# Prompt attention's values product in split single-pass form, with both kv heads in one stationary tile and the output weights of the mixer loaded later

## What is computed

```python
def attend(q, k, v, bias, key_valid, sinks):
    s = jnp.einsum('bnqhgd,bnkhd->bnhgqk', q, k).astype(jnp.float32) * (HEAD_DIM ** -0.5) + bias
    ...
    m = jnp.maximum(jnp.max(s, axis=-1, keepdims=True), sink)
    p = jnp.exp(s - m)
    w = p / (jnp.sum(p, axis=-1, keepdims=True) + jnp.exp(sink - m))
    return jnp.einsum('bnhgqk,bnkhd->bnqhgd', w.astype(v.dtype), v)
...
            c, conv_state = short_conv(cg * xi, hist, conv_w[e])
            x = x + jnp.concatenate([a, bg * c], axis=-1) @ mix_w_out[e]
```

## Time and profile before

| | us |
|---|---|
| median of 3 runs | 2050.97 |
| lowest and highest | 2050.38, 2050.98 |
| the profiled execution | 2053.99 |
| its span, first to last instruction | 2052.2 |

### The profile page before, as it was taken

The page is one execution under the profiler, slowest core; times in us unless marked ns, Lnnn a source line. Parts: engine busy times, 40 slices in busy tenths (PEclk is TensorE's granted clock), DMA queues, the critical chain, the costliest instruction groups (busy, mean ns, idle before and its releaser), DMA issues. The chain is left out here.

```text
span 2052.2 us, 34169 instructions
## 1 busy us (share of the span) xinstructions
PE 2036.8 (99%) x13819; PEld 2003.8 (98%) x13819; DVE 1468.8 (72%) x2315; ACT 811.4 (40%) x1352; POOL 533.7 (26%) x366
## 2 busy tenths in 40 slices
PE   9999999999999999999999999999999999999999
PEld 7999999999889999999999999999999999999998
DVE  4896684974666679668487789486677888576685
ACT  6343342442434334334244344243335544333343
POOL 2343232402000034223240234242320045232330
PEclk9999999999999999999999999999999999999999
DMA  6233232333221222323233223323242123323222
GB/s 156 67 83 93 73 98 68 83 98 89 60 63 42 73 68 83 93 73 98 67 83 98 72 57 83 104 62 88 78 126 79 49 60 83 94 72 93 72 57 83
DMA packets 312420, 165.22 MB, mean 81 GB/s; under 512 B 15435, under 2 KB 309527, under 8 KB 312264
## 3 DMA queue, kind: packets, MB, share of 16 engines
q1 hardware_dynamic: 307456, 157.31, 27.9%
q0 software_dynamic: 2576, 4.64, 1.0%
q10 hardware_dynamic: 2232, 1.09, 0.2%
HBM read 159.01 MB, written 4.00 MB: 79 GB/s over the span
## 5 line engine op out<-in xcount | busy, mean ns | idle before, releaser
L522 PE MATMUL psum<-xg_hi,in_hi 128*128 128x320 f32 x1952 | 609.9, 312 | 2.3 <-DVE xg_lo L1379 1.4
L523 PE MATMUL psum<-xg_lo,in_hi 128*128 128x320 f32 x1952 | 603.5, 309 | 0.0
L524 PE MATMUL psum<-xg_hi,in_lo 128*128 128x320 f32 x1952 | 603.4, 309 | 0.0
L522 PE MATMUL psum<-f_hi,f_out_hi 128*128 128x320 f32 x1408 | 436.6, 310 | 3.3 <-DVE f_out_lo L1342 1.5
L523 PE MATMUL psum<-f_lo,f_out_hi 128*128 128x320 f32 x1408 | 435.1, 309 | 0.0
L524 PE MATMUL psum<-f_hi,f_out_lo 128*128 128x320 f32 x1408 | 435.1, 309 | 0.0
L522 PEld LDWEIGHTS psum<-xg_hi,in_hi 128*128 128x128 f32 x1952 | 366.7, 188 | 9.6 <-issue 6.1
L523 PEld LDWEIGHTS psum<-xg_lo,in_hi 128*128 128x128 f32 x1952 | 366.8, 188 | 0.6
L524 PEld LDWEIGHTS psum<-xg_hi,in_lo 128*128 128x128 f32 x1952 | 366.7, 188 | 0.0
L1844 POOL TENSOR_TENSOR sums<-in_raw 128x512 f32<-128x512 f32 x72 | 101.6, 1412 | 733.0 <-DVE in_lo L1346 465.4
L1346 DVE TENSOR_TENSOR in_lo<-in_raw,in_hi 128x1024 fp32r<-128x1024 f32 x144 | 231.8, 1610 | 55.7 <-ACT in_hi L983 55.7
(11 more groups left out here) (225 smaller groups left out, 2845.5 us busy)
## 6 DMA issues: line engine op xcount, KB each, us to landing
in_raw<-in_ffn_w_gate SPq DMA_DIRECT2D x87, 512.0 KB, 4.1
in_raw<-in_ffn_w_up SPq DMA_DIRECT2D x87, 512.0 KB, 5.3
out_raw<-in_ffn_w_down SPq DMA_DIRECT2D x96, 384.0 KB, 3.3
out_raw<-in_ffn_w_down SPq DMA_DIRECT2D x32, 256.0 KB, 2.9
in_raw<-in_mix_w_in SPq DMA_DIRECT2D x14, 512.0 KB, 4.6
out<-y_nat SPq DMA_DIRECT2D x5, 512.0 KB, 3.2
in_raw<-in_mix_w_in SPq DMA_DIRECT2D x8, 256.0 KB, 4.7
out_raw<-in_mix_w_out SPq DMA_DIRECT2D x16, 128.0 KB, 2.8
```

The source lines that it names most:

```text
L522: pe.matmul(dst, w_hi, v_hi, start=first, stop=False)
L523: pe.matmul(dst, w_hi, v_lo, start=False, stop=False)
L524: return pe.matmul(dst, w_lo, v_hi, start=False, stop=last)
```

## The change

The prompt's values products take the split form. v is kept as v_hi and v_lo, turned probabilities as probs_hi0, probs_hi1 and probs_lo0, probs_lo1. ScalarE's two copies now write the high parts; VectorE subtracts them from PSUM in `probs_low(t)`, one subtraction of 512 columns and from unit 2 on one of 256, called inside bias_scores(t+1) between line 1667 and the wait for the exponentials; values(t) waits for it (probs_split). `values_low` splits v the same way during VectorE's step 2. The stationary tile is all 128 columns of v, both heads, so head i's product has 128 output partitions of which 64 are used; head 0 goes to bank 7, head 1 to bank 6, and attn_out reads 64 partitions of each with two instructions per engine instead of one. A copy v_last holds the rows to be stored. Since the new tiles lie over out_raw, the loads of output chunks 0 and 1 move behind mix chunk 8 on SP and wait for the eighth values product and the stored keys and values. The streams' units are as before.

```diff
@@ -206,7 +206,15 @@
         a_hi = over("a_hi", [P, 8, TOKENS], A_HI, F32R)
...
         t2 = over("t2", [P, 2, HALF], arena + 65792)
-        v_nat = over("v_nat", [P, NCHUNK, P], arena)
+        v_hi = over("v_hi", [P, NCHUNK, P], arena, F32R)
+        v_lo = over("v_lo", [P, NCHUNK, P], OUT_HI + 16384, F32R)
+        probs_lo0 = over("probs_lo0", [P, 2, 2, P], OUT_HI + 20480, F32R)
+        probs_lo1 = over("probs_lo1", [P, 2, P], OUT_HI + 22528, F32R)
+        v_last = over("v_last", [P, P], OUT_HI + 23552)
+        probs_hi0 = over("probs_hi0", [P, 2, 2, P], arena + 19488, F32R)
+        probs_hi1 = over("probs_hi1", [P, 2, P], arena + 21536, F32R)
         vs_nat = over("vs_nat", [T_NEW, STREAMS, P], arena + 4096)
...
@@ -343,8 +352,12 @@
         def attn_views(t, a):
...
             if t < NCHUNK:
-                dst = a[:, 0:4, t * CHUNK:(t + 1) * CHUNK].rearrange("p (a g) q -> p a g q", a=2)
-                return [(dst, psum[:, 7, 256:512].rearrange("p (a g q) -> p a g q", a=2, g=2))]
+                views = []
+                for kv in range(2):
+                    r = slice(64 * kv, 64 * kv + 64)
+                    dst = a[r, 0:4, t * CHUNK:(t + 1) * CHUNK].rearrange("p (a g) q -> p a g q", a=2)
+                    views.append((dst, psum[r, 7 - kv, 256:512].rearrange("p (a g q) -> p a g q", a=2, g=2)))
+                return views
             s = 2 * (t - NCHUNK)
@@ -493,9 +506,13 @@
             for tile, lo in ((2, 64), (3, 0), (4, 0)):
...
             start_ffn_out("ffn0", 0, 0)
-            load_ffn("ffn0", 0, 0, lambda: (load_mix_in(0), load_mix_in(1)), lambda: (load_mix_out(0), load_mix_out(1)))
+            load_ffn("ffn0", 0, 0, lambda: (load_mix_in(0), load_mix_in(1)), lambda: None)
             for c in range(2, 9):
                 load_mix_in(c)
+            sp.wait_ge(values_mm, NCHUNK)
+            sp.wait_ge(kv_stored, 16 * 4)
+            load_mix_out(0)
+            load_mix_out(1)
             start_ffn_in("ffn1", 0, 1)
@@ -758,6 +775,7 @@
             def turn_probs(t):
...
                 wait(pe, probs_copied, t)
+                wait(pe, probs_split, min(t, NCHUNK))
                 wait(pe, attn_lo, t)
@@ -774,25 +792,29 @@
...
-                pe.wait_ge(probs_copied, t + 1)
+                if t < NCHUNK:
+                    pe.wait_ge(v_split, 2)
+                    pe.wait_ge(probs_split, t + 1)
+                else:
+                    pe.wait_ge(probs_copied, t + 1)
                 wait(pe, attn_lo, t)
...
                         if t < NCHUNK:
-                            r = slice(64 * i, 64 * i + 64)
                             if b == 0:
-                                v, moving = v_nat[0:nk, max(t - 2, 0), r], probs_t0[0:nk, i].rearrange("p a q -> p (a q)")
+                                rows, c8 = slice(0, nk), max(t - 2, 0)
+                                hi, lo = (z[rows, i].rearrange("p a q -> p (a q)") for z in (probs_hi0, probs_lo0))
                             else:
-                                rows = slice(64 * i, 64 * i + nk)
-                                v, moving = v_nat[rows, t - i, r], probs_t1[rows].rearrange("p a q -> p (a q)")
-                            dst = psum[r, 7, 256:512]
+                                rows, c8 = slice(64 * i, 64 * i + nk), t - i
+                                hi, lo = (z[rows].rearrange("p a q -> p (a q)") for z in (probs_hi1, probs_lo1))
+                            last = product(psum[:, 7 - i, 256:512], v_hi[rows, c8], v_lo[rows, c8], hi, lo, first, last_block)
                         else:
...
                             dst = psum[:, 7, 256 + P * i:256 + P * i + P]
-                        last = pe.matmul(dst, v, moving, start=first, stop=last_block)
+                            last = pe.matmul(dst, v, moving, start=first, stop=last_block)
                 last.then_inc(values_mm, 1)
@@ -1212,13 +1235,12 @@
                 act.wait_ge(probs_turned, t + 1)
...
                     full = P if t > 0 else CHUNK
-                    last = act.activation(probs_t0[0:full].rearrange("p v a q -> p (v a q)"), psum[0:full, 6, :], ACT.Copy)
-                    rest = 0 if t < 2 else P
+                    last = act.activation(probs_hi0[0:full].rearrange("p v a q -> p (v a q)"), psum[0:full, 6, :], ACT.Copy)
+                    if t >= 2:
+                        last = act.activation(probs_hi1[:].rearrange("p a q -> p (a q)"), psum[:, 7, 0:2 * P], ACT.Copy)
                 else:
                     act.activation(probs_t0[:, 0].rearrange("p a q -> p (a q)"), psum[:, 6, 0:2 * P], ACT.Copy)
-                    rest = T_NEW
-                if rest:
-                    last = act.activation(probs_t1[0:rest].rearrange("p a q -> p (a q)"), psum[0:rest, 7, 0:2 * P], ACT.Copy)
+                    last = act.activation(probs_t1[0:T_NEW].rearrange("p a q -> p (a q)"), psum[0:T_NEW, 7, 0:2 * P], ACT.Copy)
                 last.then_inc(probs_copied, 1)
@@ -1267,9 +1289,11 @@
                         branch += 1
...
                     act.wait_ge(kv_turned, 1)
-                    act.activation(v_nat[:, 0:4], psum[:, 6].rearrange("p (a b) -> p a b", a=4), ACT.Copy).then_inc(kv_copied, 1)
-                    act.activation(v_nat[:, 4:7], psum[:, 7, 0:384].rearrange("p (a b) -> p a b", a=3), ACT.Copy)
-                    act.activation(v_nat[0:64, 7], psum[0:64, 7, 384:512], ACT.Copy).then_inc(kv_copied, 1)
+                    act.activation(v_hi[:, 0:4], psum[:, 6].rearrange("p (a b) -> p a b", a=4), ACT.Copy).then_inc(kv_copied, 1)
+                    act.wait_ge(out_split, OUT_CHUNK["mix"])
+                    act.activation(v_last[:, :], psum[:, 7, 256:384], ACT.Copy)
+                    act.activation(v_hi[:, 4:7], psum[:, 7, 0:384].rearrange("p (a b) -> p a b", a=3), ACT.Copy)
+                    act.activation(v_hi[0:64, 7], psum[0:64, 7, 384:512], ACT.Copy).then_inc(kv_copied, 1)
                     act.wait_ge(kv_turned, 2)
@@ -1640,6 +1664,26 @@
             def keys(t):
...
+            def probs_low(t):
+                if not 0 <= t < NCHUNK:
+                    return
+                dve.wait_ge(probs_copied, t + 1)
+                full = P if t > 0 else CHUNK
+                last = dve.tensor_tensor(probs_lo0[0:full].rearrange("p v a q -> p (v a q)"), psum[0:full, 6, :],
+                                         probs_hi0[0:full].rearrange("p v a q -> p (v a q)").bitcast(F32), ALU.subtract)
+                if t >= 2:
+                    last = dve.tensor_tensor(probs_lo1[:].rearrange("p a q -> p (a q)"), psum[:, 7, 0:2 * P],
+                                             probs_hi1[:].rearrange("p a q -> p (a q)").bitcast(F32), ALU.subtract)
+                last.then_inc(probs_split, 1)
+            def values_low():
+                dve.wait_ge(kv_copied, 1)
+                dve.tensor_tensor(v_lo[:, 0:4], psum[:, 6].rearrange("p (a b) -> p a b", a=4), v_hi[:, 0:4].bitcast(F32), ALU.subtract).then_inc(v_split, 1)
+                dve.wait_ge(kv_copied, 2)
+                dve.tensor_tensor(v_lo[:, 4:7], psum[:, 7, 0:384].rearrange("p (a b) -> p a b", a=3), v_hi[:, 4:7].bitcast(F32), ALU.subtract)
+                dve.tensor_tensor(v_lo[0:64, 7], psum[0:64, 7, 384:512], v_hi[0:64, 7].bitcast(F32), ALU.subtract).then_inc(v_split, 1)
             def bias_scores(t):
@@ -1665,6 +1709,7 @@
                 dve.tensor_reduce(negmax, rows, AX.X, ALU.max).then_inc(max_found, 1)
...
                 dve.tensor_scalar(stats[:, 0, 0:width], stats[:, 0, 0:width], -1.0, None, ALU.mult).then_inc(max_done, 1)
+                probs_low(t - 1)
                 dve.wait_ge(exp_done, 4 * (t + 1))
@@ -1770,6 +1815,8 @@
                         dve.tensor_tensor(a_lo[:, 4 + 2 * j + t, cols(half)], t2[:, t],
...
                     branch += 2
+                if step == 2:
+                    values_low()
                 if step == ATTN_FROM + 1:
...
                 if step > ATTN_FROM:
@@ -1881,7 +1928,7 @@
             pool.memset(u_p[:, :, 0:2], 0.0).then_inc(u_cleared, 1)
...
             pool.dma_start(new_k_p[0, 0].rearrange("t n d -> t (n d)"), kv_rows[:, 0]).then_inc(kv_stored, 16)
-            pool.dma_start(new_v_p[0, 0].rearrange("t n d -> t (n d)"), v_nat[:, 6]).then_inc(kv_stored, 16)
+            pool.dma_start(new_v_p[0, 0].rearrange("t n d -> t (n d)"), v_last[:, :]).then_inc(kv_stored, 16)
             pool.dma_start(new_k_s[0].rearrange("s t n d -> (s t) (n d)"), kv_rows[:, 1]).then_inc(kv_stored, 16)
```

More of the change, by code:

```diff
@@ L298, in build @@
         values_mm, attn_hi, attn_lo = sem("values_mm"), sem("attn_hi"), sem("attn_lo")
+        v_split, probs_split = sem("v_split"), sem("probs_split")
         sum_done, fast_hi, fast_split = sem("sum_done"), sem("fast_hi"), sem("fast_split")
```

## The result

The changed kernel takes 2070.4 us, the median of six runs (2067.1 to 2074.3), against 2050.7 us (2050.3 to 2054.7) for the kernel before: a ratio of 1.0091, 95% interval 1.0079 to 1.0103, so 19.7 us slower, where 7.0 were forecast. The profiled run took 2067.7 us, its span is 2065.9. One run of the first experiment (2183.0 us, at a mean clock of 0.85) is a slow one and left out of its ratio.

A forecast was written before the change was run, and what follows sets the result against it. TensorE, busy 99%, bounds the kernel, with VectorE co-bound in attention. Waits +11.3, products -3.2 and swallowed old waits -1.1 give +7.0 us on the median 2050.97: 2058.0 us, range 2054.7 to 2062.5.

The forecast's parts named there:

- The replay: Attention steps recomputed from the old times with the new terms: values(t) late in units 1 to 7, waits 11.3 us in all.
- the fit: VectorE's subtractions from PSUM: 1.04 ns a column and 0.155 us fixed, so 0.69 us for 512 columns, 0.42 for 256.
- the step "Rivals", (c): Rival: TensorE's clock falls in the attention stretch, one or two steps at the lower level, 2064 to 2070 us; chance 0.06.
- the sum: Attention stretch: waits +11.3 us, products -3.2, old waits swallowed -1.1, together +7.0 us.
- the step "TensorE's own work": values(t): products of 0.121 us and 0.09 per change of rows, 1.81 us in units 2 to 7, net -3.2 us.
- rival (a): The low split is ready before TensorE asks: no new waits, +0.1 us (-1.3 to +2.0), 2051.1 us, no change; chance 0.09.
- the second L1683: VectorE's extra low-half output instruction per attention unit, heads now in two banks: 0.34 us, plus 0.3 on ScalarE ahead.

The follow-up runs named there:

- the first experiment: The changed kernel, but values products don't wait for the low split and use the high probabilities twice, low part left out: 2053.5 us, ratio 1.0013.
- the early split: The changed kernel with VectorE doing the low split ahead of the next unit's scores instead of behind their maxima: 2059.2 us, ratio 1.0036.
- filled kernel: The changed kernel with twelve unused 256-column products on TensorE ahead of the wait for the low split, units 1 to 7: 2062.4 us, ratio 1.0055.
- the two kernels without the wait: The first experiment, 2053.5 us, and the same with one output instruction per engine for both heads, as before the change: 2051.5 us, ratio 0.9994.
- the grouped kernel: The changed kernel, complete, with both heads' 128-row products issued before both heads' 64-row ones: 2058.3 us, ratio 1.003.
- the grouped one without the wait: The first experiment with both heads' 128-row products issued before both heads' 64-row ones: 2052.1 us, ratio 1.0000.
- the experiment with the old products: The changed kernel with all its copies, splits and waits, but values products in plain fp32 on the high parts, 64 columns a head: 2066.0 us, ratio 1.0072.
- the kernel with the later position: The changed kernel with each unit's values products four row blocks later between the projection's: 2058.1 us, ratio 1.0033.

## Where the prediction was right and where it was wrong

**Right: that somebody makes TensorE wait, who, where and how often.** Seven waits on the low split were forecast, none in unit 0, 11.3 us in all; seven are there. The replay counted how late the product starts, not the idle time printed, and by that measure the trace has 11.4 us (10.3 printed): 1.82, 1.38, 2.10, 2.10, 1.37, 1.37, 1.22 against the replay's 1.5, 1.3, 2.1, 2.4, 1.5, 1.3, 1.2. That units 3 and 4 wait longest, because of the in_lo pair ahead of them, came out. The subtractions, 0.69 and 0.42 us by the fit, took 0.68 and 0.41. The moved loads cost zero, as said.

**Wrong: the step "Rivals", (c).** It gave the fall of the clock a chance of 0.06, and so the sum put the clock at nothing. Its ground was that TensorE had lived through a wait of 1.4 us, though its own replay gave new ones of up to 2.4; that one wait shows nothing about longer or more frequent ones. In the changed kernel the clock was at the lower level for 20.5 us, which costs 7.8 us, and with this the range, 2054.7 to 2062.5, missed the time. The price in (c), 2064 to 2070 for one or two steps, comes close partly by luck: 6 to 12 us on top of 2058.0 were priced, 8.0 on top of 2062.4 were measured. What the runs show is that waits take the clock down: without them, or with them filled, it stays at 1.00. They don't show that it takes a row of waits: with the early split the clock fell behind the first one. The Trainium skill, TensorE: Matmul & The Clock Gate, section "A second HAM failure mode: psum-queue depth-cycling", describes a kernel whose short idle times between groups of products make the clock swing between its levels. By that rule rival (c) would have been the likeliest case. The section gives no length of idle time, so the 8 us come from the runs here alone. The filled kernel and the one without the wait agree with it; the grouped ones, with idle times as long and less or no time at the lower level, agree only in part.

**Wrong in size: the step "TensorE's own work", the price of a change of rows.** 0.09 us was read from one spacing, the first after the change. The product behind it is late by as much again, so a change costs 0.19: 12 x 0.12 + 4 x 0.19 = 2.20, against 2.19 read in unit 4, and 1.81 in the sum. That is 0.38 us in each of six units, 2.3 us. In the old block the follower's 0.11 was counted, in the new one such a 0.10 was not, at any of the four changes. With it the products of units 2 to 7 gain 0.2 us a unit, not 0.6, or 0.3 with the gap of 0.1 ahead of the old block that the prediction left aside; steps without a wait in the kernel of the first experiment are 0.26 to 0.31 us shorter than before. The steps show it: at full clock they grew by 1.1 to 2.1 us (the filled kernel's turns: 1.40, 1.11, 1.90, 2.13, 1.16, 1.14, 1.14), where 0.5 to 1.5 was forecast.

**Wrong in size: rival (a) and the second L1683.** Its cost in the sum was 0.34 us a unit, absorbed in the replay; the trace has the two 0.43 apart (0.86 us for the pair), and measured by the two kernels without the wait it lengthens the stage by 2.8 us. In the case without the wait the replay ended at +0.1; it is +2.0 in the stage (2.0 to 2.5 by the medians), the dear end of its own bounds. That is the two sizes together.

**The whole.** Of the 18.1 us in the stage, 7.8 are the clock, 8.3 the wait at full clock (6.9 by the replay, 7.0 less 0.1), and 2.0 are the rest: 2.8 for the second output instruction, -0.8 for the products, 0.0 for the loads. At full clock the kernel would have come to 2062.4, just inside the range. The median of the changed kernel's runs is 2.7 us above its profiled run; the mean clocks they were granted go from 0.996 (2067.1 us) to 0.992 (2072.1 and 2074.3), so the spread follows the clock too.

**Open.** When a wait takes the clock down and when it doesn't. In the attention stretch of all these traces the clock falls ten times, in five kernels. Nine of the falls begin 0.8 to 2.2 us behind the end of a wait of 1.2 us or more, the tenth within the wait of 2.5 us. But 15 other waits of 1.2 us or more have no fall behind them, among them 1.95 us in the grouped kernel and 1.93 us in the grouped one without the wait. The same instructions gave mean clocks from 0.994 to 0.999 in the experiment with the old products, so something that differs between executions has a part in it. Nor does every fall need a long wait: near 1571 us in the kernel with the moved loads alone, and near 1578 us in the one with the early split, the clock is at the lower level for 3.4 us, and TensorE's longest wait there is 0.6 us. Why the grouped order loses less in each of its six runs is not shown. That the low split couldn't be had in time without making VectorE late elsewhere holds for the two ways tried.

## What to carry to other kernels

Before a change puts a wait on an engine that is busy for 99% of the span, read the timeline of the engine it will wait for, step by step: the lateness of its queue, not its busy share of 72%, is the price, and moving the work earlier or asking for it later only moved the wait to the next thing that VectorE owes. If waits of more than a microsecond are new, in each step of a loop above all, price a fall of the clock as a likely case: here it fell behind one such wait in one kernel, and others went by without a fall. Compare the granted clocks of all runs, since one profiled execution can show more or less of it than the next. And put products with the same rows of the array next to each other: the order alone was worth 0.74 us a unit here.

## What the runs showed of the hardware

- Seven waits of 1.1 to 2.0 us, one in each step of 11 to 16 us, took TensorE's granted clock to the lower level for 20.5 us; 12 products of 256 columns in each of them kept it at 1.00. In the kernel with the later position 6.8 us at the lower level came with no wait above 1.6 us, and in the one with the early split 3.4 us came behind a single wait of 1.93 us. In the grouped kernel without the wait one of 1.93 us left the clock at 1.00.
- A wait costs TensorE more than the idle time printed: with 1.95 printed the product starts 2.10 us late, and the one behind it another 0.08.
- Products of the single-pass form with 256 columns follow each other in 0.12 us. A change between 128 and 64 rows costs 0.19: 0.09 ahead of the first product and 0.10 ahead of the second.
- Two 64-row products in different row halves, next to each other in the queue, run at the same time: six of them in 0.56 us (548.50 to 549.06), with both changes in it. With 128-row products between them they don't. The Trainium skill, TensorEngine Tiling (Array Packing), section Key Properties, says that tiles in different parts of the array run in parallel, and these rows agree.
- One more instruction a unit on VectorE, 0.42 us for 64 rows as for 128 (L1728 after, L1683 before), lengthened the stage by 2.8 us though VectorE is busy for 72% of the span.
